# A new order for the attention items of both layers in a hybrid attention and MoE block

## The reference, cut to what matters

```python
(q_a, k_a, v_a, q_i, k_i, w_i, q_b, k_b, v_b, c_q, c_kv, k_r) = jnp.split(h @ w_in, splits, axis=-1)
o_a = dsa_attention(q_a, k_a, v_a, q_i, k_i, w_i)     # index scores, top 64 keys, then softmax
o_b = diff_attention(q_b, k_b, v_b, lam, lam_init, subln)   # p[0] - lam * p[1], then a norm
q_c = (rms_norm(c_q, q_norm) @ w_uq)...;  kv = (rms_norm(c_kv, kv_norm) @ w_ukv)...
o_c = mla_attention(q_nope, q_rope, k_nope, k_rope, v_c)    # latent attention, 8 heads
o = jnp.concatenate([o_a, o_b, o_c], axis=-1);  h = h + o @ w_out
```

## Time and profile before

| | us |
|---|---|
| median of 3 runs | 1617.63 |
| lowest, highest | 1617.40, 1618.18 |
| the profiled execution | 1613.17 |
| its span, first to last instruction | 1611.1 |
| PE busy in it | 1569.2 (97%) |
| DVE busy | 1261.6 (78%) |
| ACT busy | 1035.2 (64%) |

### The profile page before, as it was taken

The page is one execution under the profiler, slowest core; times in us unless marked ns, Lnnn a source line. Parts: engine busy times, 40 slices in busy tenths (PEclk is TensorE's granted clock), DMA queues, the critical chain, the costliest instruction groups (busy, mean ns, idle before and its releaser), DMA issues.

```text
span 1611.1 us, 20849 instructions
## 1 busy us (share of the span) xinstructions
PE 1569.2 (97%) x7246; PEld 1270.4 (79%) x7246; DVE 1261.6 (78%) x1550; ACT 1035.2 (64%) x1334; POOL 58.6 (4%) x128
## 2 busy tenths in 40 slices
PE   7989999999999999999999999999999999999996
PEld 6867788887786788888888888888888888888885
DVE  6477655555557779889899899899899889889995
ACT  5445544443345357777787687787778678678774
POOL 2200000000212000000000000000000000000000
PEclk9978999999997799999999999999999999999999
DMA  7502545453351139999999999899899899999992
GB/s 280 191 1 105 211 174 184 181 190 133 118 187 56 54 138 382 339 353 363 335 354 359 326 352 363 319 355 368 326 351 366 320 359 361 348 325 369 357 359 93
DMA packets 181784, 431.10 MB, mean 268 GB/s; under 512 B 3808, under 2 KB 10336, under 8 KB 181728
## 3 DMA queue, kind: packets, MB, share of 16 engines
q1 hardware_dynamic: 180720, 428.01, 73.4%
q10 hardware_dynamic: 1008, 2.36, 0.4%
HBM read 429.31 MB, written 1.05 MB: 267 GB/s over the span
## 4 chain that ended last, share of the span: by engine, by line
PE 95%; DVE 3%; ACT 1%; issue 1%; POOL 0%; DMA 0%; DVEq 0%; SPq 0%; POOLq 0%
PE pair L802 49%; PE work L802 32%; PE pair L867 3%; PE work L778 3%; PE work L1042 2%; PE pair L778 2%; PE work L940 2%; PE work L789 1%; PE work L1056 0%; PE work L1057 0%; DVE arena L1485 0%; DMA h<-in_x 0%; PE pair L870 0%; DVE hnT_lo L1434 0%; DVE arena L1502 0%
## 5 line engine op out<-in xcount | busy, mean ns | idle before, releaser
L1426 DVE TENSOR_TENSOR w_lo<-ring,w_hi 128x1024 fp32r<-128x1024 f32 (+3 forms) x810 | 965.2, 1213 | 215.9 <-ACT w_hi L1137 210.1
L1137 ACT ACTIVATE w_hi<-ring 128x1024 fp32r<-128x1024 f32 (+3 forms) x810 | 844.5, 1053 | 348.7 <-PE pair L802 176.4
L802 PE MATMUL pair<-w_hi,hnT_hi 128*128 128x512 f32 x1120 | 448.1, 400 | 2.9 <-DVE hnT_lo L1434 2.6
L802 PE MATMUL pair<-w_hi,hnT_lo 128*128 128x512 f32 x1120 | 442.4, 395 | 0.0
L802 PE MATMUL pair<-w_lo,hnT_hi 128*128 128x512 f32 x1120 | 442.3, 395 | 0.0
L802 PEld LDWEIGHTS pair<-w_hi,hnT_hi 128*128 128x128 f32 x1120 | 210.3, 188 | 51.6 <-DVE hnT_lo L1434 3.5
L802 PEld LDWEIGHTS pair<-w_hi,hnT_lo 128*128 128x128 f32 x1120 | 210.3, 188 | 51.3
L802 PEld LDWEIGHTS pair<-w_lo,hnT_hi 128*128 128x128 f32 x1120 | 210.4, 188 | 47.9
L802 PE MATMUL work<-w_hi,hidT_hi 128*128 128x512 f32 x552 | 219.5, 398 | 2.6 <-DVE hidT_lo L1673 1.4
L802 PE MATMUL work<-w_hi,hidT_lo 128*128 128x512 f32 x552 | 218.2, 395 | 0.0
L802 PE MATMUL work<-w_lo,hidT_hi 128*128 128x512 f32 x552 | 218.2, 395 | 0.0
(11 more groups left out here) (184 smaller groups left out, 1093.0 us busy)
## 6 DMA issues: line engine op xcount, KB each, us to landing
ring<-in_moe_w_gate SPq DMA_DIRECT2D x56, 2048.0 KB, 8.9
ring<-in_moe_w_up SPq DMA_DIRECT2D x56, 2048.0 KB, 9.1
ring<-in_moe_w_down SPq DMA_DIRECT2D x56, 2048.0 KB, 8.4
ring<-in_dense_w_gate SPq DMA_DIRECT2D x7, 2048.0 KB, 7.8
ring<-in_dense_w_up SPq DMA_DIRECT2D x7, 2048.0 KB, 7.7
ring<-in_dense_w_down SPq DMA_DIRECT2D x7, 2048.0 KB, 7.8
ring<-in_w_in SPq DMA_DIRECT2D x4, 2048.0 KB, 9.6
ring<-in_w_out SPq DMA_DIRECT2D x4, 2048.0 KB, 9.5
```

The costliest lines, as they stand in the source:

```text
L802: mm = pe.matmul(b, lhs[x_part][k + kk], w[w_part][:, kk, :], start=(first and kk == 0 and i == 0), stop=(last and kk == 1 and i == 2))
L1137: return act.activation(o, i, ACT.Copy)
L1426: dve.tensor_tensor(lo, raw, hi.bitcast(F32), ALU.subtract).then_inc(lo_done, 1)
```

## The change

Only the two lists in `LISTS` change. Each holds the same items as before, each once. Kept here are the places that the prediction speaks of; "..." stands for the rest of a list.

```diff
 LISTS = ("""
-... U.mla.0.1 SP.17 MQ.1.0 U.mla.0.2 PI.1 SP.18 SP.19 SP.20 SP.21 PI.0 PK.0 R.b.0 R.i.0 PK.1 R.i.1 BT.0 TP.mla.0.1 U.mla.1.3
-... U.idx.0.3 IT.1 TK.0.0 O.mla.1.2 TK.0.1 R.b.1 U.idx.1.0 TK.0.2 U.idx.1.1 U.idx.1.2 BT.1 U.idx.1.3 U.diff.1.2
-TK.0.3 U.diff.0.0 AT.0 U.diff.1.1 CB.diff.1.2 AT.1 TK.0.4 TP.diff.1.2 TK.1.0 ...
-... U.mla.1.1 U.mla.1.0 TK.1.5 TK.1.6 O.diff.1.0 O.dsa.0.1 TK.1.7 D1.0 TP.diff.1.3 TP.mla.1.1
-O.diff.1.3 TP.mla.1.0 U.dsa.1.0 U.dsa.1.1 CB.mla.1.1 D2.0 CB.mla.1.0 O.mla.1.0 O.mla.1.1 D1.1 TP.dsa.1.0
-OT.0.1 TP.dsa.1.1 OT.0.0 SP.22 SP.23 CB.dsa.1.0 D2.1 O.dsa.1.0 CB.dsa.1.1 O.dsa.1.1 SP.24 SP.25 SP.26 SP.27
-WO.0.0 OT.1.0 OT.1.1 WO.0.1 NF1.0 NF2.0 WO.1.0 SP.28 SP.29 SP.30 WO.1.1 XF.0.1 NF1.1 XF.0.0 NF2.1
+... U.mla.0.2 PB.0 MQ.1.0 CB.mla.0.2 MQ.1.1 MK.1.0 SP.15 TP.mla.0.2 U.mla.0.1 U.mla.0.0 U.mla.0.3 MK.1.1 O.mla.0.2 ...
+SP.17 SP.18 PI.0 CB.mla.0.0 SP.19 SP.20 SP.21 CB.mla.0.3 PI.1 SP.22 TP.mla.0.1 PK.0 U.mla.1.0 R.a.1 TP.mla.0.0
+O.mla.0.1 U.mla.1.2 CB.mla.1.2 TP.mla.0.3 R.i.0 PK.1 O.mla.0.0 O.mla.0.3 KIT.0 ... SP.23 R.i.1
+SP.24 TP.mla.1.0 TP.mla.1.2 IT.0 U.mla.1.3 ... U.idx.0.0 U.idx.0.1 TP.mla.1.3 U.idx.0.2 U.idx.0.3 BT.0 U.mla.1.1 TK.0.0 ...
+CB.diff.0.0 U.idx.1.0 BT.1 TP.diff.0.1 U.idx.1.1 ... CB.diff.0.3 U.idx.1.2 TP.diff.1.3 O.diff.0.0 U.idx.1.3 TP.diff.0.3 U.dsa.0.0
+... TP.diff.1.0 TK.1.1 TK.1.2 OT.0.0 OT.0.1 TK.1.3 TK.1.4 TK.1.5 TK.1.6 TP.diff.1.1 SP.25 TK.1.7 SP.26 SP.27
+U.dsa.1.0 O.diff.1.0 U.dsa.1.1 O.diff.1.1 D1.1 WO.0.0 WO.0.1 CB.dsa.1.1 D2.1 TP.dsa.1.0 TP.dsa.1.1 CB.dsa.1.0
+NF1.0 O.dsa.1.0 O.dsa.1.1 NF2.0 OT.1.1 OT.1.0 SP.28 SP.29 XF.0.1 XF.0.0 WO.1.0 WO.1.1 SP.30 NF1.1 NF2.1
 """, """
-N1.0 N2.0 X.0.0 X.0.1 SP.0 SP.1 SP.2 SP.3 N1.1 N2.1 PC.0 C1.0 X.1.1 C2.0 X.1.0 SP.4 CT.0 PC.1 ...
-... U.mla.0.2 ... PI.0 CB.mla.0.0 PK.0 ... U.mla.1.2 PK.1 O.mla.0.3 O.mla.0.0 SP.23 SP.24 R.b.0 TP.mla.1.2
-TP.mla.0.2 R.a.1 R.i.1 BT.0 IT.0 U.mla.1.3 KIT.0 U.mla.1.0 U.diff.0.1 ...
-... TK.1.6 O.diff.1.1 SP.27 TK.1.7 U.dsa.1.0
-U.dsa.1.1 O.diff.1.3 D1.1 CB.dsa.1.1 WO.0.0 WO.0.1 LR TP.dsa.1.0 CB.dsa.1.0 D2.1 TP.dsa.1.1 O.dsa.1.0
-O.dsa.1.1 XF.0.1 NF1.0 OT.1.1 OT.1.0 XF.0.0 SP.28 SP.29 NF2.0 WO.1.0 WO.1.1 SP.30 NF1.1 XF.1.1 XF.1.0 NF2.1
+N1.0 N2.0 X.0.0 X.0.1 SP.0 SP.1 SP.2 SP.3 SP.4 N1.1 SP.5 PC.0 N2.1 R.kr.0 X.1.1 C1.0 X.1.0 PC.1 R.kr.1 C2.0
+CT.0 C1.1 ...
+... U.mla.1.0 O.mla.0.1 SP.19 SP.20 O.mla.0.3 PI.0 U.mla.1.3
+SP.21 TP.mla.0.2 PK.0 R.i.0 SP.22 TP.mla.1.0 U.mla.1.1 U.mla.1.2 PK.1 KIT.0 SP.23 CB.mla.1.0 IT.0 CB.mla.1.2
+... TP.diff.0.2 U.idx.1.0 TK.0.6 BT.1 U.idx.1.1 TP.diff.0.3 AT.1 U.idx.1.2 ... U.idx.1.3 ...
+TP.diff.1.1 TP.diff.1.3 TK.1.5 TK.1.6 TK.1.7 U.dsa.1.0 U.dsa.1.1 O.diff.1.3 CB.diff.1.0 WO.0.0 TP.dsa.1.0
+O.diff.1.1 SP.25 TP.diff.1.0 CB.dsa.1.1 CB.dsa.1.0 SP.26 O.dsa.1.0 O.diff.1.0 TP.dsa.1.1 D1.1 SP.27 D2.1
+WO.0.1 O.dsa.1.1 XF.0.0 OT.1.1 OT.1.0 NF1.0 WO.1.0 NF2.0 SP.28 SP.29 SP.30 WO.1.1 XF.0.1 XF.1.0 NF1.1 XF.1.1
+NF2.1 RT.0 RT.1
 """)
```

More of the change, by code:

```diff
@@ L42 @@
[L42 to L46, removed]
@@ L58 @@
[L58 to L62, removed]
@@ L63 @@
[L63 to L67, removed]
@@ new lines @@
+CB.mla.0.2 MQ.1.1 MK.1.0 SP.15 TP.mla.0.2 U.mla.0.1 U.mla.0.0 U.mla.0.3 MK.1.1 O.mla.0.2 CB.mla.0.1 SP.16
+SP.17 SP.18 PI.0 CB.mla.0.0 SP.19 SP.20 SP.21 CB.mla.0.3 PI.1 SP.22 TP.mla.0.1 PK.0 U.mla.1.0 R.a.1 TP.mla.0.0
+O.mla.0.1 U.mla.1.2 CB.mla.1.2 TP.mla.0.3 R.i.0 PK.1 O.mla.0.0 O.mla.0.3 KIT.0 R.a.0 CB.mla.1.0 SP.23 R.i.1
+SP.24 TP.mla.1.0 TP.mla.1.2 IT.0 U.mla.1.3 R.b.0 KIT.1 O.mla.1.0 CB.mla.1.3 U.idx.0.0 U.idx.0.1 TP.mla.1.3
+U.idx.0.2 U.idx.0.3 BT.0 U.mla.1.1 TK.0.0 U.diff.0.2 TK.0.1 O.mla.1.2 O.mla.1.3 TK.0.2 TP.mla.1.1 CB.diff.0.2
@@ new lines @@
+IT.1 AT.0 TK.0.3 CB.mla.1.1 U.diff.0.1 R.b.1 TK.0.4 U.diff.0.0 TP.diff.0.2 CB.diff.0.1 O.mla.1.1 TK.0.5
+CB.diff.0.0 U.idx.1.0 BT.1 TP.diff.0.1 U.idx.1.1 O.diff.0.2 TP.diff.0.0 U.diff.1.3 TK.0.6 O.diff.0.1
+U.diff.0.3 CB.diff.1.3 TK.0.7 CB.diff.0.3 U.idx.1.2 TP.diff.1.3 O.diff.0.0 U.idx.1.3 TP.diff.0.3 U.dsa.0.0
+O.diff.1.3 U.dsa.0.1 O.diff.0.3 CB.dsa.0.0 U.diff.1.2 TK.1.0 D1.0 CB.dsa.0.1 AT.1 TP.dsa.0.0 TP.dsa.0.1
+U.diff.1.0 CB.diff.1.2 O.dsa.0.0 U.diff.1.1 TP.diff.1.2 D2.0 O.dsa.0.1 CB.diff.1.0 CB.diff.1.1 O.diff.1.2
@@ new lines @@
+MQ.0.1 QC.1.1 KV.1.0 KV.1.1 U.mla.0.0 U.mla.0.1 QC.1.0 CB.mla.0.1 CB.mla.0.0 SP.11 TP.mla.0.0 SP.12 U.mla.0.3
+R.c.1 PB.1 R.a.1 MQ.1.1 U.mla.0.2 SP.13 SP.14 MK.1.0 PB.0 O.mla.0.0 SP.15 SP.16 TP.mla.0.1 MK.1.1 MQ.1.0
+CB.mla.0.2 SP.17 PI.1 CB.mla.0.3 TP.mla.0.3 SP.18 U.mla.1.0 O.mla.0.1 SP.19 SP.20 O.mla.0.3 PI.0 U.mla.1.3
+SP.21 TP.mla.0.2 PK.0 R.i.0 SP.22 TP.mla.1.0 U.mla.1.1 U.mla.1.2 PK.1 KIT.0 SP.23 CB.mla.1.0 IT.0 CB.mla.1.2
+O.mla.1.0 R.i.1 SP.24 O.mla.0.2 TP.mla.1.1 TP.mla.1.3 U.idx.0.0 U.idx.0.1 CB.mla.1.3 CB.mla.1.1 R.b.0
@@ new lines @@
+O.mla.1.3 TP.mla.1.2 U.idx.0.2 R.b.1 U.idx.0.3 KIT.1 TK.0.0 TK.0.1 BT.0 IT.1 U.diff.0.2 U.diff.0.3 TK.0.2
+R.a.0 CB.diff.0.2 TK.0.3 CB.diff.0.3 O.mla.1.1 TK.0.4 TK.0.5 O.mla.1.2 TP.diff.0.2 U.idx.1.0 TK.0.6 BT.1
+U.idx.1.1 TP.diff.0.3 AT.1 U.idx.1.2 U.diff.0.1 AT.0 TK.0.7 U.diff.1.2 CB.diff.0.1 O.diff.0.2 U.diff.0.0
+CB.diff.1.2 CB.diff.0.0 O.diff.0.3 TP.diff.0.1 U.idx.1.3 O.diff.0.1 TK.1.0 TP.diff.1.2 TP.diff.0.0 LR
+O.diff.1.2 U.dsa.0.1 U.dsa.0.0 O.diff.0.0 D1.0 U.diff.1.1 TP.dsa.0.1 CB.dsa.0.0 TP.dsa.0.0 CB.dsa.0.1 TK.1.1
```

19 lines of the change are left out of this document (6 added, 13 removed).

## The result

The change makes the kernel slower. The median of 9 executions is 1624.94 us (1617.08 to 1628.92) against 1613.4 (1611.98 to 1618.18) of the kernel before, ratio 1.0056 with an interval of 1.0041 to 1.0071: some 9 us (the medians differ by 11.5). The forecast set out from a median of 1617.6, the first three executions of the kernel before; the nine give 1613.4, so measured from there the forecast of -4.8 would have been 1608.6, and the miss is larger than 1624.9 against 1612.8. The profiled execution takes 1621.72 us (span 1619.8), 8.55 more than that of before.

The account below looks back on a forecast made before the run. PE, busy 97%, was taken to bound the kernel, with DVE as the other bound in the mixers; -0.6 (layer 0), -3.7 (layer 1) and -0.5 (exit) gave -4.8, from 1617.6 to 1612.8 us, range 1605 to 1622.

Parts of the forecast that it names:

- The half stretch: Small items behind PK.1 at half clock: 25 to 32 us in each layer instead of 34 and 41.
- Rival A: The clock holds in the mixers because the 4.51 us wait is gone: -12.3 with the exit, 1605.3 us; chance 0.13.
- my fourth sign of being wrong: A clock that falls between the projections would show the prediction wrong; no size given.
- Moved splits: SP.19, SP.23 and SP.27 at new places in the lists were to cost nothing.
- Latent work ahead: Latent work moved ahead of PK.1: 6.0 us in layer 0, 8.2 in layer 1; removes 10.2 and 13.9 behind it.
- Index units apart: Tile 1's index units standing apart behind PK.1: 6.3 us for 2.6 in layer 0, +3.7; layer 1 -2.4.
- Waits: PE's waits: 3.0 us saved in layer 0; in layer 1 POOL's 1.19 goes and 1.1 is saved at the entry.
- DVE as the bound: PK.1 to the maximum of U.dsa.1.0: DVE work 49.1 and 42.7 us at share 0.82; layer 0 -0.6, layer 1 -3.7.
- rival B: DVE's share does not rise, PE waits at each TP: +5.6 with the exit, 1623.2 us; chance 0.20.
- Tail of layer 0: WO.0.0 and WO.0.1 now hide the search, as in layer 1; sparse units apart add about 1 us, +1.0.
- Exit: Layer 0's exit: XF.0 before WO.1.0 removes a 2.6 us wait, but XF.1 still holds the dense product; -0.5.
- Layer 1: Layer 1's mixer ends at 569.5 us, -3.7, with a new PE wait of some 5.6 us before TP.dsa.1.0.

Follow-up runs that it names:

- five products per transpose: Kernel before, its 4.51 us wait filled with idle products, plus five before each transpose of a differential or sparse unit of layer 0: 1611.31 us, ratio 0.9993.
- its partner: The run with the first list alone: changed list of layer 0 with the old list of layer 1; 1625.83 us, ratio 1.0071 against the kernel before.
- new head: Layer 0's changed list up to PK.1, in several runs; joined to the old rest, with layer 1 old: 1630.93 us, ratio 1.0118 against the kernel before.
- old head and new rest: Layer 0's old list up to PK.1, then the remaining items in changed order, layer 1 old: 1616.26 us, ratio 1.0016 against the kernel before.
- old tail: Changed list of layer 0 up to O.diff.0.3, then the old order, layer 1 old: 1629.39 us, ratio 1.0115 against the kernel before.
- filled: Twelve idle products in the first dense product's wait for XF.1, on top of the filled wait behind PK.1: 1615.84 us, ratio 1.0015 against the kernel before.

## Why the prediction was wrong

The profiled executions of all 20 kernels, set side by side, show what the forecast of the clock lacked (one execution each, layer 0 only):

| PE behind PK.1 of layer 0 | runs | the clock falls |
|---|---|---|
| a wait of 1.5 us or more | 11 (old and new order) | 0.1 to 3.7 us after PE stopped |
| two waits of 0.5 and 1.1 us | 2 | one 7, one 29 us after PK.1 |
| no wait over 1 us before the fall (one run has 1.40 us just at it) | 6 | 13 to 31 us after PK.1 |
| the same, five products per transpose | 1 | not in the mixer |

How long it then stays down varies from run to run, as told above.

**The half stretch (25 to 32 us instead of 34).** The step that failed. I took the distance between PK.1 and the fall as given and moved work out of the stretch behind it. It is no place in time: a wait sets it off, and work taken out is followed by other work at the same clock. It came at +6 us: 14 + 24 us at half clock in the profile, 55 in its partner, and over all executions 103 us for 91. By the forecast's terms (-10.2, +3.7, -3.0, +1.0) the stretch from PK.1 to the end of WO.1.1 was to shrink by 8.5 us; it shrank by 0.6. Rival A named the mechanism (waiting makes the clock fall) and I asked of it only whether the 4.51 us wait goes; it went, and a wait of 1.69 took its place, 9 us earlier. The Trainium skill, page "TensorE: Matmul & The Clock Gate", section "HAM oscillation — how this bites in real kernels", which I cited for A, gives idle gaps as the cause. The runs agree for the waits above, and differ where PE was never idle: with narrow items alone the clock fell as well. It did so even ahead of PK.1, my fourth sign of being wrong: in 4 of the 12 profiled runs with the new head the clock fell at 60 to 62 us for 3.4 us, among the latent units that the new head puts together or right behind them, with PE never waiting; in none of the 8 with the old head. In the run with the first list alone:

```profile
61.00:65.00 4.00, 4.00 (x17) 3.41 (x17) 2.83 (x8) 3.87 (x15) 0.00 (x0) 0.58 0.80 265
```

**Moved splits ("nothing").** Wrong. I asked of SP.23 only what it holds in the weight ring, not what DVE's splits do to POOL beside them: 1.73 us on R.i.1. The trace of before could have told, in layer 1, where the same two splits stand behind PK.1. The last step of R.b.0 takes 1.18 us there beside them, where a step of this size takes 0.32 alone, and the wait of 1.19 us in the earlier trace rows ends with it:

```profile
484.68 0.32 POOL L687 TENSOR_TENSOR arena<-rope_c,rope_s 128x64 f32<-128x64 f32 x1
485.08 1.18 POOL L688 TENSOR_TENSOR arena<-rope_c,rope_s 128x64 f32<-128x64 f32 x1
```
```profile
484.85 2.50 DVE L1426 TENSOR_TENSOR w_lo<-ring,w_hi 128x1024 fp32r<-128x1024 f32 x2
```

I had put that wait down to R.i.1 behind R.a.1, and read past the step's length.

**Latent work ahead.** The size on PE was right: 6.0 forecast, 6.0 between the runs with old and new head. (The profiled execution of before, from which I counted, has PK.1 at 76.8, 1.3 us earlier than the middle of its kind; hence 83.9 for 82.8.) What it does to the items behind was missed: R.i.1 starts from PK.1, and KIT.1 now has 4 us of PE work ahead of it instead of 10.

**Index units apart (+3.7).** Right in kind, too large for the index units; that all units together come to it is luck. I added up PE's rows from each start to the next, less waits, with time at half clock divided by 1.8. So reckoned, units behind PK.1 take 19.9 us in the kernel before, 23.6 with the old head and new rest (+3.7), 19.2 in the changed kernel; putting only the four index units together takes off 2.3 in either order. In the changed kernel the four of tile 1 are 1.13 three times and 2.07 once, 5.5 us for the 6.3 of the forecast:

```profile
106.52 1.13 PE L867 MATMUL pair<-arena 64*128 64x256 f32 x4
...
115.36 2.07 PE L867 MATMUL pair<-arena 64*128 64x256 f32 x4
```

With transposes and outputs the work behind PK.1 is 43.0 us before, 48.0 with the old head and new rest, and 41.8 in the changed kernel: 6 went ahead of PK.1, but 5 came with the new rest, 3.7 of them in the units. It fell hardly at all.

**Waits.** The 4.51 us of the earlier trace rows are gone; all waits between PK.1 and WO.1.1 were 7.5 us before and are 4.4 after: 3.1, as forecast, but the new ones stand where they cost clock. In layer 1 the wait for POOL was to go (1.19) and is 0.86; one of 1.40 for DVE came with the fall at 510.

**DVE as the bound.** DVE's work was right (48.7 us, forecast 49.1), its share was 0.76, not 0.82, and the model itself was wrong: PE is busy 60.8 of 64.5 us there, and over 4 us less work for DVE brought 0.7. In layer 1 the share was 43.6 of 55.1, 0.79, and the wait of 5.6 us before TP.dsa.1.0 didn't come. The number that decides (0.79) was met, and rival B's sum (+5.6) is near the profiled loss by luck, not by its mechanism: PE waited less than before, it ran at half clock.

**Tail of layer 0 (+1.0).** Its form was right: from TP.dsa.1.0 (152.0) to WO.1.0 (158.5) are 6.5 us, as layer 1 had 7. Going back to the old tail was dearer.

**Exit (-0.5).** The wait moved and stayed, 2.99 for the 2.6 of the earlier trace rows, as forecast. The dense part was 2.3 us longer by a fall of the clock. Of 19 profiled runs with this wait 10 show such a fall, the new exit and the old among them; filled, it was gone. I had priced a wait by its length alone.

**Layer 1 (-3.7).** The mixer gained 1.6 in the profile, the router gave it back, and alone the list is some 2.6 us slower (0.6 to 4.4). The 17 us to the fall became 11. Here, too, I took one execution for all: with the old second list the mixer of layer 1 stands at half clock for 31 us in 9 of the 16 profiled runs, 34 in two and 41, as in the one I read, in five; with the new one for 37.5 to 41 in all four.

**The range** (1605 to 1622) had its upper end from rival B. It held no term for a clock lost earlier than before. The 17 us more at half clock of the run with the first list alone (108 against 91) are 17 x 0.38 = 6.5 us, which would have put the upper end that much higher, with 1624.9 inside.

## What to carry over

Before pricing an order by what runs at which clock, list every wait that the new order gives PE behind its last large product, with the engine that ends it; a wait of 1.7 us, with the time at half clock behind it, cost some 9 here. A move ahead of a product brings the work behind it closer to the product's own consumers: count what is left to cover their chain, POOL's included, and what DVE does beside POOL. And where executions differ, compare spans at equal mean clock; one profile per kernel shows one of several courses.

## What was not expected of the hardware

Idle products in a wait of PE save more than they cost: eight of 0.233 us brought back 9.4 us, with KIT.1 starting within 0.05 us of where it did. 17.5 us of idle products between narrow items kept 2.4 GHz throughout a mixer that otherwise has 24 us at 1.2 GHz, and the end didn't move. POOL's 0.49 and 0.34 us steps became 1.36 and 1.20 beside DVE's splits. And with the new items behind the same wait of 1.5 to 1.7 us, the clock was back after 3.4 us in two profiled runs, after 14 in two and after 55 in two.
